# The first norm of a two-block transformer kernel: order of the ada chunks, place of the sums of squares, and engine of the small loads

## The reference

```python
mx = (jax.nn.silu(c) @ w_ada[l] + b_ada[l])[:, None, :]
sh1, sc1, ga1, sh2, sc2, ga2 = jnp.split(mx, 6, axis=-1)
mc = jax.nn.silu(c_ctx) @ w_ada[l] + b_ada[l]
csh1, csc1, cga1, csh2, csc2, cga2 = jnp.split(mc, 6, axis=-1)
pc = modulate(rmsnorm(ctx, g_norm1[l]), csh1, csc1) @ w_in[l]     # h * (1 + scale) + shift
...
px = modulate(rmsnorm(x, g_norm1[l]), sh1, sc1) @ w_in[l]
```

## Time and profile before

| | us |
|---|---|
| median of three runs | 2169.39 (2168.69 to 2171.74) |
| profiled execution | 2166.3 |
| its span | 2164.4 |
| TensorE busy | 1996.4 (92%) |
| VectorE busy | 733.9 (34%) |
| ScalarE busy | 470.2 (22%) |
| mean granted TensorE clock | 0.959 of full speed |

### The profile page before, as it was taken

The page is one execution under the profiler, slowest core; times in us unless marked ns, Lnnn a source line. Parts: engine busy times, 40 slices in busy tenths (PEclk is TensorE's granted clock), DMA queues, the critical chain, the costliest instruction groups (busy, mean ns, idle before and its releaser), DMA issues.

```text
span 2164.4 us, 19621 instructions
## 1 busy us (share of the span) xinstructions
PE 1996.4 (92%) x7415; PEld 921.1 (43%) x7415; DVE 733.9 (34%) x1355; ACT 470.2 (22%) x845; POOL 12.6 (1%) x17
## 2 busy tenths in 40 slices
PE   6899999999899999999997997899997859999997
PEld 3544545544364444344433442344444334444443
DVE  3606205521231111111113695210212255455554
ACT  3211114420211110010112006530003222323223
POOL 0000000000000000000000000000000020000000
PEclk7999999999999999999998997999998969999999
DMA  9111443113238999999980211111200048878862
GB/s 371 28 66 39 173 177 136 39 59 117 78 122 349 422 417 419 422 422 422 423 345 18 72 66 39 40 39 62 72 22 0 0 151 289 296 273 288 293 233 78
DMA packets 151110, 399.03 MB, mean 184 GB/s; under 512 B 9284, under 2 KB 75156, under 8 KB 142868
## 3 DMA queue, kind: packets, MB, share of 16 engines
q1 hardware_dynamic: 144636, 393.40, 48.0%
q10 hardware_dynamic: 6424, 4.94, 0.7%
HBM read 396.23 MB, written 2.10 MB: 184 GB/s over the span
## 4 chain that ended last, share of the span: by engine, by line
PE 88%; DVE 4%; ACT 3%; issue 1%; DMA 1%; SPq 0%; DVEq 0%; ACTq 0%
PE bank L1529 49%; PE bank L1852 10%; PE bank L2099 6%; PE bank L1876 5%; PE bank L1827 3%; PE bank L1898 3%; PE bank L2121 3%; DVE SM L582 1%; PE bank L574 1%; PE bank L1980 1%; PE bank L2065 1%; PE bank L1605 1%; PE bank L1727 1%; PE bank L1560 1%; DMA weight_slots<-in_expert_w_up 1%
## 5 line engine op out<-in xcount | busy, mean ns | idle before, releaser
L1529 PE MATMUL bank<-H,weight_slots 128*128 128x512 f32 (+1 forms) x1088 | 450.0, 574 | 13.7 <-ACT H L620 12.5
L1529 PEld LDWEIGHTS bank<-H,weight_slots 128*128 128x128 f32 x1088 | 208.9, 193 | 252.6 <-issue 247.3
L1529 PE MATMUL bank<-R,weight_slots 128*128 128x512 f32 x576 | 249.1, 593 | 4.4 <-DVE R L1158 2.1
L1529 PEld LDWEIGHTS bank<-R,weight_slots 128*128 128x128 f32 x576 | 109.0, 190 | 141.6 <-issue 134.6
L1852 PE MATMUL bank<-weight_slots,SM 128*64 128x512 f32 x640 | 141.8, 593 | 6.8 <-DVE xT L1221 6.8
L2099 PE MATMUL bank<-weight_slots,SM 128*64 128x512 f32 x512 | 136.3, 622 | 5.6 <-DMA weight_slots<-in_expert_w_up 5.6
L1471 DVE TENSOR_TENSOR xT<-xT,bank 128x512 f32<-128x512 f32 x136 | 91.6, 686 | 78.8 <-PE bank L1529 78.8
L1876 PE MATMUL bank<-weight_slots,SM 128*64 128x512 f32 x384 | 111.6, 594 | 0.0
L1529 PE MATMUL bank<-R 128*128 128x128 f32 (+2 forms) x784 | 103.3, 287 | 3.2 <-ACT R L874 2.1
L1529 PEld LDWEIGHTS bank<-R 128*128 128x128 f32 x784 | 94.2, 195 | 7.1 <-issue 4.6
L1852 PEld LDWEIGHTS bank<-weight_slots,SM 128*64 128x64 f32 x640 | 45.4, 137 | 100.1 <-issue 86.7
(11 more groups left out here) (386 smaller groups left out, 2057.0 us busy)
## 6 DMA issues: line engine op xcount, KB each, us to landing
weight_slots<-in_w_up_e SPq DMA_DIRECT2D x24, 2048.0 KB, 12.7
weight_slots<-in_w_down_e SPq DMA_DIRECT2D x24, 2048.0 KB, 20.8
weight_slots<-in_w_in SPq DMA_DIRECT2D x18, 2048.0 KB, 10.2
weight_slots<-in_w_gate_e SPq DMA_DIRECT2D x16, 2048.0 KB, 11.8
weight_slots<-in_expert_w_gate SPq DMA_DIRECT2D x32, 1024.0 KB, 10.0
weight_slots<-in_expert_w_up SPq DMA_DIRECT2D x32, 1024.0 KB, 11.7
R<-in_expert_w_down SPq DMA_DIRECT2D x32, 1024.0 KB, 8.3
weight_slots<-in_w_ada SPq DMA_DIRECT2D x12, 2048.0 KB, 10.3
```

What stands on the lines that cost most here:

```text
L1529: ins = nc.tensor.matmul(dst, lhsT, rhs, start=(i == 0), stop=(i == len(pairs) - 1))
```

## The change

It has four pieces. The list `ADA_CHUNK` makes the first two loads and products the scale chunks (2 and 3) and the next two the shift chunks (0 and 1); `ada_bias` writes each to its own place in `mods`. TensorE runs both first products, both their sums, then the sums of squares of x and the fold, and only then the other two chunks. VectorE takes the context reciprocal first, forms the gains after two chunks, scales the context, takes the x reciprocal, handles the shift chunks, and scales x; ScalarE's context biases wait for the shift instead of for the gains. The nine small loads are issued by SyncE ahead of ada4. Chunks 4 to 11 keep their order.

```diff
+ADA_CHUNK = (2, 3, 0, 1, 4, 5, 6, 7, 8, 9, 10, 11)
...
-            W.append((f"ada{s}", cols(w_ada, 512 * s), "ada_mm", s + 1))
+            W.append((f"ada{s}", cols(w_ada, 512 * ADA_CHUNK[s]), "ada_mm", s + 1))
...
+            def small_weights():
+                sp.dma_start(rowb[0:1, 0:16], A["b_gates"].rearrange("a g h -> a (g h)")).then_inc(sem("rowb_in"), 16)
...
+                for src in (w_in[:, OFF_G:OFF_BR], A["w_router"][0], A["w_in_2"][0, :, OFF_F2:OFF_F2 + 8], A["router_group_w_2"][0], A["router_expert_w_2"][0]):
+                    n = src.shape[1]
+                    sp.dma_start(wsmall[:, :, c:c + n], src.rearrange("(k p) n -> p k n", p=P)).then_inc(sem("wsmall_in"), 16)
+                    c += n
+
             for n, (name, src, free, value) in enumerate(W):
+                if n == 2 * NSLOT:
+                    small_weights()
...
-            act.dma_start(rowb[0:1, 0:16], A["b_gates"].rearrange("a g h -> a (g h)")).then_inc(sem("rowb_in"), 16)
...
-                act.dma_start(wsmall[:, :, c:c + n], src.rearrange("(k p) n -> p k n", p=P)).then_inc(sem("wsmall_in"), 16)
-                c += n
-
-            act.wait_ge(sem("gains1"), 2)
             for k in range(KD):
+                act.wait_ge(sem("mods"), 6 + 2 * (k // 4))
                 act.wait_ge(sem("rms_out"), norm_out("nc", k))
...
+            root_inverse("nc", TC, std[:, T:T + TC], rstd[:, T:T + TC])
             ada(0, ada_part0)
             ada(1, ada_part0)
             ada_bias(0)
-            root_inverse("nc", TC, std[:, T:T + TC], rstd[:, T:T + TC])
-            ada(2, ada_part0)
             ada_bias(1)
-            ada(3, ada_part0)
-            ada_bias(2)
-            ada_bias(3)
-
-            dve.wait_ge(sem("mods"), 8)
+            dve.wait_ge(sem("mods"), 4)
...
+            scaled("nc", ctxT, T, TC, 1)
+            root_inverse("n1", T, std[:, 0:T], rstd[:, 0:T])
+            ada(2, ada_part0)
+            ada(3, ada_part0)
+            ada_bias(2)
+            ada_bias(3)
+            dve.wait_ge(sem("rms_out"), KD + 1)
+            scaled("n1", xT, 0, T, 0)
...
             ada(0)
             ada(1)
             ada_sum(0, ada_part0)
+            ada_sum(1, ada_part0)
+            wide_sum(pe, "n1", take(PART_BANK, "rms_part", WIDE["n1"]), take(0, "rms_std", NORMS["n1"] + 1))
             ada(2)
-            ada_sum(1, ada_part0)
             ada(3)
             ada_sum(2, ada_part0)
             ada_sum(3, ada_part0)
-            wide_sum(pe, "n1", take(PART_BANK, "rms_part", WIDE["n1"]), take(0, "rms_std", NORMS["n1"] + 1))
```

More of the change, by code:

```diff
@@ L443, in _ @@
             sp.dma_start(vpack[0:124, 2, :], A["conv_dw_w_2"].rearrange("a w (k n) -> (a w k) n", n=P)).then_inc(sem("vecs_in"), 16)
+            def small_weights():
+                sp.dma_start(rowb[0:1, 0:16], A["b_gates"].rearrange("a g h -> a (g h)")).then_inc(sem("rowb_in"), 16)
+                sp.dma_start(rowb[0:1, 16:24], A["fox_bf_2"]).then_inc(sem("rowb_in"), 16)
+                sp.dma_start(rowb[0:1, 24:28], A["router_group_b_2"]).then_inc(sem("rowb_in"), 16)
+                sp.dma_start(rowb[0:1, 28:44], A["router_expert_b_2"]).then_inc(sem("rowb_in"), 16)
+                c = 0
+                for src in (w_in[:, OFF_G:OFF_BR], A["w_router"][0], A["w_in_2"][0, :, OFF_F2:OFF_F2 + 8], A["router_group_w_2"][0], A["router_expert_w_2"][0]):
+                    n = src.shape[1]
+                    sp.dma_start(wsmall[:, :, c:c + n], src.rearrange("(k p) n -> p k n", p=P)).then_inc(sem("wsmall_in"), 16)
+                    c += n
             for n, (name, src, free, value) in enumerate(W):
+                if n == 2 * NSLOT:
+                    small_weights()
                 if n >= NSLOT:
@@ L953, in ada_bias @@
                 for i in range(2):
-                    nc.vector.tensor_tensor(mods[:, 4 * s:4 * s + 4, i], PS[6 + s % 2][:, 0:8].rearrange("p (c m) -> p c m", m=2)[:, :, i],
-                                            v("b_ada", 4 * s, 4), ALU.add).then_inc(sem("mods"), 1)
+                    c = 4 * ADA_CHUNK[s]
+                    nc.vector.tensor_tensor(mods[:, c:c + 4, i], PS[6 + s % 2][:, 0:8].rearrange("p (c m) -> p c m", m=2)[:, :, i],
+                                            v("b_ada", c, 4), ALU.add).then_inc(sem("mods"), 1)
             def root_inverse(name, width, std_, rstd_):
@@ L975, in _, with scaled @@
             dve.wait_ge(sem("gains1"), 2)
[L976 to L979, removed]
+            def scaled(name, src, c, width, i):
                 dve.wait_ge(sem("rstd"), NORMS[name] + 1)
```

## The result

The changed kernel takes 2148.64 us in the median (2147.98 to 2151.03), the kernel before 2169.30 beside it (2168.69 to 2171.74): a ratio of 0.9905, 95% interval 0.9887 to 0.9922, or 20.7 us faster. The forecast had 17.0 us, 2152.4, and a range down to 2149; the direction was right, the size too small.

The account below looks back on a forecast made before the run. TensorE work bounds the kernel (88% of the chain of waits). Key products start at 43.95 instead of 61.54: 8.3 (loads) plus 9.3 (order) is 17.6, less 0.55 for the clock gives 17.0, so 2152.4 us; range 2149 to 2160.

Parts of the forecast that it names:

- each duration behind the first ada_sum: Run-up to the key products: squares 1.92, fold 1.12, x reciprocal 3.35, later ada products 1.92 and sums 1.05 each.
- the hidden work: Context scaling, reciprocal, small loads and x biases run beside the path; small loads have over 60 us cover, cost 0.
- nothing waits anew behind 105: After the key products: the forecast would be wrong if a new wait appeared there; thin product unstalled near 128.
- Up to the first ada_sum nothing changes: TensorE's front, before the norm's sums: same times as in the old profile, first ada_sum from 28.15 to 29.20.
- The 0.55 charged for the clock's return at the products: Start of key products: low clock lasts 4.4 us instead of 3.3, 1.1 us more at half speed, costing 0.55.
- ScalarE's price holds: Nine small loads moved to SyncE: issuing them there needs some 9 us, if they cost the same as on ScalarE.
- the split into 8.3 for the loads and 9.3 for the order: Key products' start 17.6 us earlier: 8.3 from moving small loads off ScalarE, 9.3 from the new order.
- Rival 3: Only the issues count: run-up to the key products no shorter, gain 8.3 us, 2161.1; chance 0.05.
- Rivals 1 and 2 (half speed): Run-up at half speed after the norm: gain 13.5, 2155.9, chance 0.28; or from 28 on: 10.5, 2158.9, 0.08.
- The new late event: What would be late next before the key products: the key weights, landing near 40.9, 3 us early.

Follow-up runs that it names:

- the front filler: Changed kernel plus two 128x512 matmuls, result never read, in TensorE's pause before the first ada product: 2148.23 us, ratio 0.9909.

## Why the prediction was too small

**Where it was right.** The place (the start of the key products), the direction, each duration behind the first ada_sum, the hidden work (context scaling, reciprocal, small loads, x biases), and that nothing waits anew behind 105. With the same clock in front as in the trace of before, its start was right to 0.04 us (43.91 against 43.95). That closeness is partly luck: in that trace the ada products began at 23.52, 0.6 later than the forecast's 22.89. In the run of the order alone, with 5.34 us of ada products from 22.70, the last two ada_sums began at 38.49, 0.7 before the forecast's 39.15.

**The step that failed: the sum's terms.** (1) "Up to the first ada_sum nothing changes: it runs 28.15 to 29.20." This left the two first ada products as in the trace of before, 5.34 us at a clock that had fallen at 23.9. That came from one trace and was not even named as a choice. In both traces of the changed kernel they took 3.75 and 3.64, the first ada_sum ran from 26.37, and the start is 42.01: 1.9 us more gain. (2) The 0.55 charged for the clock's return at the products: it came back 2.9 us after the start, not 4.4; the distance grows from 19.5 to 19.75 instead of shrinking, 0.8 us. That is the 2.7 us between the forecast's 17.0 and the traces' 19.75. (3) The range: its lower end let only the clock at the key products vary, with 1 us for waits and 0.7 for the spread of runs. The clock in front of the ada products was no term of it, nor were the low stretches behind 100 us, which moved the profiled gain by 7 us between four pairs. A range around one trace's sum had to be wider on both sides.

The traces show the first two terms in the head; the totals are too coarse to confirm them. The run with the small loads behind the x biases started at 43.91 and still had a median gain of 20.9, and behind the thin product the changed kernel's first trace is 4.4 us longer than that of before (2149.1 - 126.06 against 2164.4 - 145.81). The median missed the range by 0.4 us.

**The step that was wrong in kind.** "ScalarE's price holds" and the split into 8.3 for the loads and 9.3 for the order. The nine issues do not cost 8.9 us wherever they stand: they took 8.9, 12.9, 13.4 and 20.2 us in four runs in which the big loads ran beside them for some 6, 10, 11 and 23 us. In the changed kernel they took 15.7 on SyncE, where the prediction had some 9; it cost nothing there, as nothing on the path stood behind them. So with the issues left on ScalarE a faster run-up is largely lost in that wait, and the order alone was worth 5.2, not 9.3. The loads alone were worth what the split said (8.3 by the start), but 15.4 beside the new order (57.43 - 42.01). The sum was right because both parts were done together. Rival 3 had looked at the issues as a fixed price too.

**What was weighed as a rival.** Rivals 1 and 2 (half speed) did not come; the clock was 1.00 from 20 to 41. The new late event was foreseen as the key weights, with 3 us to spare; it is the fourth ada chunk (35.35), and one step behind it k.

**What stays open.** Of the unprofiled executions only the time and the mean clock of the whole span are on record. In the changed kernel the two go together: 2151.03 at 0.964 (the profiled one), 2149.04 at 0.965, 2148.23 at 0.966, 2147.98 at 0.967. So that its median lies 2.4 below its first profiled execution fits less time at the low clock; where in the span was not seen. In the kernel before they do not: both profiled executions took 2166.30, at 0.959 and 0.957, and others took 2172.48 at 0.957 and 2167.20 at 0.964. Why its median lies 3 above its profiled execution stays open. Nor is it known what decides the clock in front of the ada products. Of sixteen traces without the front filler, the first two products took 3.6 to 3.9 us in nine and 5.1 to 5.3 in seven; the kernel before's order has both (two and three traces), the new order too (seven and four).

## What to carry to other kernels

A DMA issue is not a fixed price: on an engine that also computes, put it where nothing on the path stands behind it, above all while megabyte loads are in flight. Undo each part by itself before believing a split: two parts here gave 7.4 and 5.2 alone and 20.5 together, because the issues that one part moves took 20.2 us instead of 8.9 once the other part let them begin earlier. When a gain of a few microseconds is read from two traces, compare the starts of the same instruction in both, and look in the granted clock's rows for what the rest may be; a start held back by a memset tells whether it moves.

## What the runs showed of the hardware that I had not expected

- The issue of a narrow weight load took 0.58 us on SyncE once the big loads were over, and up to 5.99 us on ScalarE while 2 MB loads by SyncE were in flight; holding two of these back brought the last one down to 1.25. SyncE was held too: in the changed kernel one of its narrow issues took 4.63 us from 48.93, with its own big loads in flight.
- In that time the DMA engines moved 354 GB/s, against 387 without the narrow loads. ScalarE's queue got 171 packets of a narrow row through in a microsecond beside the big loads, and 1435 without them.
- Two traces of the same kernel had their slow stretches at the same places. A memset of 0.91 or 1.76 us in front of all first loads took those in 300:340 out of the changed kernel (1.00 instead of 0.87); in the kernel before the short one left them in place. The profiled difference of the two kernels moved by 7 us.
